# A mixture-of-experts decoder step on one core: when the second and third expert's weights are sent for, in what pieces, and how many filler products stand ahead of the first transposes

## What is computed

```python
def hier_moe(x2, w_rg, b_rg, w_re, b_re, w_e_in, w_e_out):
    """x2 (T, D). Top-1 expert group, then top-2 experts inside it."""
...
    def expert_block(args):
        xb, e = args
        gu = xb @ w_e_in[e]
        gt, up = jnp.split(gu, 2, axis=-1)
        return (jax.nn.silu(gt) * up) @ w_e_out[e]
...
    x = layer_norm(ALPHA * x + mix, ln1_g[l], ln1_b[l])
...
    x = layer_norm(ALPHA * x + ffn, ln2_g[l], ln2_b[l])
```

## Time and profile before

| | us |
|---|---|
| median of 3 runs (1563.1 to 1563.88) | 1563.75 |
| the profiled execution, own time | 1562.75 |
| its span in the profile | 1560.7 |

### The profile page before, as it was taken

The page is one execution under the profiler, slowest core; times in us unless marked ns, Lnnn a source line. Parts: engine busy times, 40 slices in busy tenths (PEclk is TensorE's granted clock), DMA queues, the critical chain, the costliest instruction groups (busy, mean ns, idle before and its releaser), DMA issues.

```text
span 1560.7 us, 35074 instructions
## 1 busy us (share of the span) xinstructions
PE 1473.1 (94%) x14561; PEld 1193.4 (76%) x14561; DVE 698.0 (45%) x1269; ACT 455.3 (29%) x875; POOL 188.4 (12%) x360
## 2 busy tenths in 40 slices
PE   7999999999999999999999999989978887898977
PEld 7999999999988999999988879875544443454442
DVE  5766576676789663323354335684111111111104
ACT  4533635453422462213244343211100010010102
POOL 1100000000000000000000000003333232233323
PEclk9999999999999999999999999999999999899999
DMA  5222435534458422262355472949999999999996
GB/s 207 70 92 81 132 112 163 150 116 131 125 210 305 144 82 95 81 236 81 94 189 216 148 286 85 387 187 393 420 422 422 421 420 423 410 385 421 419 423 253
DMA packets 87683, 368.28 MB, mean 236 GB/s; under 512 B 13904, under 2 KB 37664, under 8 KB 73088
## 3 DMA queue, kind: packets, MB, share of 16 engines
q1 hardware_dynamic: 81408, 357.38, 60.6%
q0 software_dynamic: 6144, 8.95, 1.6%
HBM read 344.82 MB, written 29.31 MB: 240 GB/s over the span
## 4 chain that ended last, share of the span: by engine, by line
PE 75%; DMA 17%; DVE 4%; issue 1%; ACT 1%; SPq 1%; POOL 0%; POOLq 0%; DVEq 0%; ACTq 0%
PE ps L671 37%; DMA arena<-in_w 16%; PE ps L1216 8%; PE ps L815 5%; PE ps L1235 4%; PE ps L924 3%; PE ps L1068 3%; PE ps L905 3%; PE ps L766 1%; PE ps L763 1%; PE ps L935 1%; PE ps L958 1%; PE ps L1200 1%; PE ps L1008 1%; PE ps L756 1%
## 5 line engine op out<-in xcount | busy, mean ns | idle before, releaser
L1216 PE MATMUL ps<-arena,xT 128*32 128x256 f32 x4096 | 254.3, 400 | 60.8 <-DMA arena<-in_w 60.3
L1216 PEld LDWEIGHTS ps<-arena,xT 128*32 128x32 f32 x4096 | 131.7, 114 | 158.9 <-DMA arena<-in_w 41.8
L1774 DVE TENSOR_TENSOR wl<-raw,wh 128x1024 fp32r<-128x1024 f32 x151 | 183.4, 1222 | 151.7 <-ACT wh L1307 151.1
L671 PE MATMUL ps<-xh,wh 128*128 128x272 f32 x1136 | 243.2, 295 | 1.4 <-ACT tmp L1319 0.7
L671 PE MATMUL ps<-xh,wl 128*128 128x272 f32 x1136 | 234.9, 288 | 0.0
L671 PE MATMUL ps<-xl,wh 128*128 128x272 f32 x1136 | 234.2, 288 | 0.0
L671 PEld LDWEIGHTS ps<-xh,wh 128*128 128x128 f32 x1136 | 179.0, 188 | 11.8 <-issue 9.2
L671 PEld LDWEIGHTS ps<-xl,wh 128*128 128x128 f32 x1136 | 178.5, 188 | 0.0
L671 PEld LDWEIGHTS ps<-xh,wl 128*128 128x128 f32 x1136 | 177.4, 189 | 0.0
L1307 ACT ACTIVATE wh<-raw 128x1024 fp32r<-128x1024 f32 x151 | 157.9, 1055 | 36.1 <-DMA raw<-in_slabs 19.7
L2522 DVE TENSOR_TENSOR hbuf<-sg,ps 128x128 f32<-128x128 f32 x64 | 18.4, 288 | 295.8 <-ACT sg L1626 295.6
(11 more groups left out here) (456 smaller groups left out, 2364.1 us busy)
## 6 DMA issues: line engine op xcount, KB each, us to landing
arena<-in_w SPq DMA_DIRECT2D x96, 2048.0 KB
raw<-in_slabs SPq DMA_DIRECT2D x151, 512.0 KB, 4.4
bc<-acs_dram SPq DMA_DIRECT2D x16, 512.0 KB, 5.8
hs<-in_h SPq DMA_DIRECT2D x16, 512.0 KB, 5.4
out_h_sample<-hs SPq DMA_DIRECT2D x16, 512.0 KB, 4.1
kv<-in_kT SPq DMA_DIRECT2D x8, 1024.0 KB, 5.0
kvx<-in_vc SPq DMA_DIRECT2D x2, 2048.0 KB, 9.8
yld<-ybuf_dram SPq DMA_DIRECT2D x4, 1024.0 KB, 8.3
```

What stands on the lines that cost most here:

```text
L671: r = nc.tensor.matmul(ps[:, 2 * (ub % 2) + half, 0:HT], w[:, s, col], x[:, koff + kk, half * HT:half * HT + HT], start=first and kk == 0 ...
L1216: r = nc.tensor.matmul(ps[QS * c:QS * c + QS, 2, 0:2 * FQ], xT[:, s, kk % 2, kk // 2 * QS:kk // 2 * QS + QS], arena[:, at_:at_ + 2 * FQ], ...
L1774: v.tensor_tensor(wl[:, s], raw[:, s], wh[:, s].bitcast(F32), ALU.subtract).then_inc(w_lo, 1)
```

## The change

It does three things. The first matrices of the experts 1 and 2 are sent for in eight transfers of 512 KB (4 KB in each partition) each, in place of two of 2 MB; the four of a half count on the same semaphore, so that the waits of `gate_up` on these two places ask for three times 16 more. The wait for the gathers 0 and 1 ahead of the third expert's matrix is gone. And the `turn_over(10)` ahead of the first `turn_x` is a `turn_over(4)`.

```diff
+PIECES = 4
...
+            def fetch1_pieces(n_):
+                for half in range(2):
+                    for piece in range(PIECES):
+                        col = half * (W1S // 2) + piece * (W1S // 2 // PIECES)
+                        at_ = w1_at[n_ % 3] + col
+                        sp_.dma_start(arena[:, at_:at_ + W1S // 2 // PIECES], A["w1"][n_][:, col:col + W1S // 2 // PIECES]
+                                      ).then_inc(w1_in[n_ % 3][half], 16)
...
             sp_.wait_ge(w_free, RING + DENSE)
-            fetch1(1)
+            fetch1_pieces(1)
             store_x1(TT - 1)
-            for s in range(2):
-                sp_.wait_ge(Z[f"g_in{s}"], 16)
-            fetch1(2)
+            fetch1_pieces(2)
             sp_.wait_ge(Z["eid_v"], 1)
...
-            turn_over(10)
+            turn_over(4)
...
-                        pe.wait_ge(w1_in[b_ % 3][kk // (KT // 2)], 16 * (b_ // 3 + 1) if ob is None else ix(16 * (W1_USES + 1), ob, 16))
+                        pe.wait_ge(w1_in[b_ % 3][kk // (KT // 2)], 16 * (b_ // 3 + 1 + (PIECES - 1 if b_ % 3 else 0)) if ob is None
+                                   else ix(16 * (W1_USES + 1), ob, 16))
```

## The result

| | before | changed |
|---|---|---|
| median of 9 runs each, us | 1563.1 (1561.24 to 1564.48) | 1567.0 (1565.57 to 1568.84) |
| profiled execution, own time, us | 1562.75 | 1565.84 |
| its span, us | 1560.7 | 1563.8 |

The ratio is 1.0024, with a 95% interval of 1.0014 to 1.0034: the change makes the kernel some 3.8 us slower (2.2 to 5.3). I had forecast 1563.4, 0.4 less than the 1563.75 of before, with a range of 1560.6 to 1566.4; the result lies above it.

The account below looks back on a forecast made before the run. The weight stream, begun for good after `gate_up(1)`, bounds the kernel. TensorE's -0.7 or +1.0, less 0.3 of queue and 0.3 of uneven engines, gives -1.3 or +0.4, middle -0.4: 1563.75 becomes 1563.4 us, range 1560.6 to 1566.4.

Parts of the forecast that it names:

- What bounds the kernel: The weight stream sets the end; expert 3's transfers wait for `gate_up(1)`, and TensorE passes any later shift on.
- The hold taken away: Expert 2's matrix, issued behind the last store, is in by about 1056.5; the DMAs' idle time moves and is not filled.
- queue and uneven engines: Ahead of expert 3's transfers: 0.3 us of queue no longer hiding a wait, 0.3 us from a lagging DMA engine catching up.
- The gathers in the new traffic: Gather 0 behind 4 KB weight rows waits seven rows, 1.1 us more, landing near 1054.0 in place of 1052.9.
- A: TensorE's clock rises at 1056.4 as before; `gate_up(0)` ends at 1059.3 against 1060.0: -0.7 us.
- B: TensorE's clock stays low to 1059.8; `gate_up(0)` ends at 1061.0: +1.0 us; held a little likelier.
- The clock: With four fillers TensorE idles before `gate_up(0)`, and products cost almost twice as much at the low clock; bounds -2.4 to +2.2.
- Rival 1: Small rows don't help gather 0, which lands at 1057.0: +2.0 to +3.7 us, 1565.8 to 1567.4; chance 0.12.
- Rival 3: The 512 KB pieces don't overlap, each paying its start and landing alone: some 5 us later, 1569; chance 0.01.
- rival 2: The idle nine microseconds are really won: 1555.3, chance 0.02; in its small form -3.7 us, 1560.1, chance 0.07.
- four signs of being wrong: Gather 0 after 1057; pieces much over 10.5 us; expert 3's transfers before 1062 or after 1067; stream after 1066 not full.

Follow-up runs that it names:

- e1: The changed kernel with ten filler products in place of four; ratio 1.0015 against the kernel before, +2.3 us.
- e2: The kernel before with four filler products in place of ten, nothing else changed; ratio 1.0005, +0.8 us.
- e3: The kernel before with only the wait for gathers 0 and 1 taken away (16 KB rows, ten fillers); ratio 1.0030, +4.7 us.
- e4: The kernel before with only the transfers in pieces (wait for the gathers and ten fillers kept); ratio 1.0007, +1.1 us.
- e5: The kernel before, with the first half of expert 2's first matrix sent at once, the second held until gather 0 landed; ratio 0.9996, -0.6 us.
- e6: e5 with four filler products ahead of the first transposes in place of ten; ratio 0.9998 against the kernel before, -0.3 us.
- e7: e6 with four more filler products behind the first sorting product; ratio 0.9990 against the kernel before, -1.6 us.
- e8: e1 with pieces of half the size (2 KB rows, 16 transfers of 256 KB a matrix); one run, 1564.4 us.
- e9: The changed kernel with sixteen filler products in place of four; ratio 1.0017 against the kernel before, +2.7 us.
- e10: The kernel before with only e7's four more filler products behind the first sorting product; ratio 1.0000.
- e11: e7 with seven filler products ahead of the first transposes in place of four; ratio 1.0000 against the kernel before.
- e12: The changed kernel with only the wait for gathers 0 and 1 put back (pieces and four fillers stay); ratio 1.0005 against the kernel before, +0.8 us.

## Why the prediction was wrong

**What bounds the kernel: right, and shown.** I held that the stream begins for good with the end of `gate_up(1)`, and that a shift there passes through. In the profiles, times in us from the gather's issue, the end of `gate_up(1)`, and what is left of the span behind it; the last column is the difference to before by the ratio of all runs:

| kernel | issue of gather 0 to first transposes | TensorE waited for it | `gate_up(0)` | issue to end of `gate_up(1)` | `gate_up(1)` ends | span less that | runs |
|---|---|---|---|---|---|---|---|
| before | 4.89 | 0 | 3.77 | 14.4 | 1064.6 | 496.1 | |
| changed | 5.67 | 3.1 | 5.04 | 16.5 | 1068.3 | 495.5 | +3.8 |
| e1 | 5.75 | 0.7 | 5.10 | 16.6 | 1066.3 | 497.1 | +2.3 |
| e2 | 2.79 | 0.3 | 5.05 | 13.6 | 1063.8 | 495.6 | +0.8 |
| e3 | 6.77 | 1.7 | 6.13 | 18.7 | 1068.5 | 495.3 | +4.7 |
| e4 | 4.89 | 0 | 3.91 | 14.5 | 1064.2 | 497.0 | +1.1 |
| e5 | 4.89 | 0 | 3.71 | 14.2 | 1065.9 | 495.2 | -0.6 |
| e6 | 3.11 | 0.6 | 6.46 | 15.3 | 1066.6 | 495.6 | -0.3 |
| e7 | 3.42 | 0.8 | 6.10 | 15.3 | 1066.1 | 495.6 | -1.6 |
| e8 | 6.17 | 1.1 | 4.96 | 16.9 | 1066.9 | 495.4 | one run |
| e9 | 5.70 | 0 | 3.70 | 14.9 | 1065.2 | 497.2 | +2.7 |
| e10 | 3.86 | 0 | 3.70 | 13.0 | 1063.3 | 496.7 | 0.0 |
| e11 | 3.71 | 0 | 3.71 | 12.9 | 1063.0 | 494.8 | 0.0 |
| e12 | 2.83 | 0.3 | 6.41 | 15.0 | 1064.5 | 496.8 | +0.8 |

What is left of the span stays within 2.4 us, while the end of `gate_up(1)` moves by 5.5. One execution starts its expert part more than 2 us sooner or later than another (the last store is issued between 1043.4 and 1045.7), whatever the kernel, and the profiled execution can be far from the median of its kernel (e11 3.8 us below it, e2 2.4, e3 and e9 2.1); so a size of one or two microseconds goes by the last column, and the others only tell where it can lie. That this is the path is shown by one edit each way: the hold taken out (e3) makes this end and the time later, the hold put back (e12) brings both back.

**The hold taken away: right as far as it went.** The idle time moved and was not filled (0.06 share from 1059.5 to 1069.5); e5 fills half of it and wins nothing. For my 0.6 us of queue and uneven engines there is no test: the two profiles differ by 0.6 in what lies behind `gate_up(1)` (496.1 and 495.5), but that column scatters by 2.4. The matrix in pieces was in by about 1059.3, later than my 1056.5: the expert part began 0.65 us later, and from 1046 to 1051 the DMAs, at a share of 0.97, moved 322 GB/s and not 418. What that costs was not measured apart from the rest; with the hold in place the pieces cost 1.1 us, not told apart from nothing (e4).

**The gathers in the new traffic: the step that failed.** "If it is a number of rows, 7 x 0.16 = 1.1 us; I take that." It was 5.58 less 2.7, 2.9 us. The queue of the gathers, 1051.9 to 1056.2 of the changed kernel, doesn't stand in the list at all; in the next 0.8 us it moves its 0.05 MB:

```profile
q1 hardware_dynamic: 486, 1.77, 102.1%
```

```profile
q1 hardware_dynamic: 74, 0.26, 83.1%
q0 software_dynamic: 46, 0.05, 17.5%
```

I had the wait of the earlier trace rows as 2 us to the first byte and 2 more to the last and then scaled both with the rows, without a row for it. The first part does not scale: with rows of 2, 4 and 16 KB the first data came 2.7, 2.6 and 2.5 us later than without load (e8, e1, e3). The rule of the Trainium skill, "DMA: Bandwidth & Descriptors", section "Queues, rings and completion order", is that an engine takes turns packet by packet. If a packet holds as many rows in each of these kernels, the first part would by it have had to shrink with the rows as well, and the measurement disagrees with it here.

**What the gather's wait makes of the sum.** Counted from the gather's issue, so that the later start of this execution drops out: I had the transposes 3.9 us behind it (1054.1 less 1050.24), and they came after 5.67, 1.8 later. `gate_up(0)` was to take 4.3 us (A) or 6.0 (B) and took 5.04, between the two. It was to end 9.1 (A) or 10.8 (B) us after the issue, 9.8 before, and ended after 11.9. The middle of A and B misses this by 1.9, and 1.8 of it are the gather. With the 1.8 us added, the forecast difference of -0.4 becomes +1.4. The other 2.4 of the measured +3.8 (interval 2.2 to 5.3) stay open: the profile of the changed kernel, 1.2 us faster than its median, does not show them, and e3's `gate_up(0)` of 6.13 us shows only that the low clock can cost another microsecond.

**The clock: the mechanism right, its size not foreseeable from one profile.** The clock stayed low past 1056.4, as in case B (from 1047.8 to 1061.5). Over all profiles, `gate_up(0)` took 3.70 to 3.91 us in the six in which TensorE did not wait for the gather, and 4.96 to 6.46 in the eight in which it did; but not by the length of the wait: 0.3 us of it stand beside 6.41 (e12) and 5.05 (e2), 3.1 beside 5.04. e2 and e12 have the same four fillers and a gather landed after the same 2.8 us. The fillers left out are, by the runs, worth 3.8 - 2.3 = 1.5 us without the hold, and with it, by e12 and e4, -0.3; neither difference is clear of the intervals.

**The rivals.** Rival 1 happened in its effect: I gave it +2.0 to +3.7 and 0.12; its chance was too small, since the one wait that the trace of before showed spoke for it and my scaling had no row at all. Its premise, that small rows don't help, is half right: the gather landed 2.9 us later than without load and not 4.1, and against e3, e1 lands its gather 1.5 us sooner and is some 2.4 us faster. That the measured 1567.0 lies within its 1565.8 to 1567.4 is therefore in part luck. Rival 3 did not happen (e4), nor rival 2: the wait on `gate_up(1)` only grew, and e5 wins nothing. Of my four signs of being wrong three were seen: gather 0 landed after 1057 (1057.45), the matrix in pieces took some 12 us (the store's data were through near 1047, the matrix was in at 1059.3), and expert 3's transfers were issued after 1067 (1068.55).

## What to carry to other kernels

Idle time of a queue is worth filling only if the transfer behind it can start sooner; ask first which buffer that one writes and who still reads it. A small transfer that an engine waits for should find the DMA engines free: smaller rows beside it took at most 1.5 of some 4 us off its wait, and holding the big transfer until it has landed cost nothing measurable here. A wait measured under one load is not to be scaled to another without a row for it; its parts may not scale alike. The number of filler products, between 4 and 16, made no difference here that is clear of the intervals, though single profiles differ by up to 2.8 us in one block: such a choice is made by many runs.

## What the runs showed of the hardware that was not expected

The first data of an indirect DMA under a full weight stream came 4.4 to 4.6 us after its issue with rows of 2, 4 and 16 KB, against 1.9 in empty engines; what this fixed part is remains open. In e5 the engines were at a share of 1.00 until about 1053, 1.3 us after the gather's issue at 1051.69, and its first data still came after 1.9 us: in this profile load at the issue that had ended when the data was due did not delay it. The queues in 1051.7 to 1053.5 of e5, and then in 1053.5 to 1054.2:

```profile
q1 hardware_dynamic: 46, 0.61, 78.8%
```

```profile
q0 software_dynamic: 48, 0.05, 21.8%
```

TensorE's clock fell near 1048 to 1051 in all the kernels and rose between 1053 and 1063. Profiles with the same products and nearly the same waits differ by more than the effects sought: after the gather's issue the clock rose at 6.7 us in e2 and at 9.5 in e12. An edit that lives on a warm clock, as e7 and e11, has to be judged by many runs.
